# Three stages of one fused kernel: the root turned by transfers, splits ahead of squares, pooled low parts on GpSimd, two heads' values in streams of 512 columns

## What is computed

```python
def multiscale_pool(u):            # 4 groups of 128 channels, windows 2, 4, 8, 16
    ...
    return window_sum / count - ug

def second_block(x, norm_mix, w_in, ...):
    for l in range(DEPTH_2):
        h = rmsnorm(x, norm_mix[l])
        proj = h @ w_in[l]
        q, k, v, r, lr_f, lr_b, u, g_a, g_b = jnp.split(proj, split_points, axis=-1)
        ...
        o_fwd = gla_chunked(qh, kh, vh, af, include_diag=True)     # 4 heads, chunks of 64
        ...
        o = o * lax.rsqrt(jnp.mean(o * o, axis=-1, keepdims=True) + EPS)
        o = (o * gla_norm * jax.nn.silu(r)).astype(x.dtype)
        y_a = o @ w_branch_gla[l]
        pooled = multiscale_pool(u)
        y_b = jnp.einsum('blgc,gcd->blgd', pooled, w_pool_group[l]).reshape(bsz, length, D_MODEL)
        merged = jax.nn.sigmoid(g_a) * y_a + jax.nn.sigmoid(g_b) * (y_b * pool_scale[l])
        x = x + merged @ w_out[l]
        ...
```

## Time and profile before

| | |
|---|---|
| Median of 3 runs | 1809.94 us (1809.89 to 1810.12) |
| The profiled execution | 1811.46 us, its span 1810.2 us |
| Granted clock of the core | 0.999 |
| PE busy | 1792.0 us, 99% |
| DVE busy | 1274.1 us, 70% |
| ACT busy | 812.8 us, 45% |
| POOL busy | 291.7 us, 16% |

### The profile page before, as it was taken

One profiled execution on the slowest core, in us unless ns is written; L12 is line 12 of the kernel. 1 busy time (PEld: TensorE's weight loads), 2 busy tenths in 40 slices (PEclk: granted clock), 3 DMA queues, 4 the chain that ended last, 5 costly groups with the idle time before them and its releaser, 6 DMA issues.

```text
span 1810.2 us, 21907 instructions
## 1 busy us (share of the span) xinstructions
PE 1792.0 (99%) x8576; PEld 1459.0 (81%) x8580; DVE 1274.1 (70%) x1687; ACT 812.8 (45%) x1072; POOL 291.7 (16%) x236
## 2 busy tenths in 40 slices
PE   9999999999999999999999999999999999999998
PEld 7888888888877668888888878788888888888886
DVE  7896868686879865767686887666447455856757
ACT  6753534343434863444343454566323343323334
POOL 0004000000145874000000041111001321011012
PEclk9999999999999999999999999999999999999999
DMA  6233253443234003452524222222332223431512
GB/s 234 94 117 115 72 186 79 133 133 98 65 99 140 25 1 117 136 166 47 183 54 159 61 92 76 65 70 71 96 114 82 94 93 140 140 117 47 175 59 76
DMA packets 153222, 186.39 MB, mean 103 GB/s; under 512 B 8576, under 2 KB 121344, under 8 KB 153120
## 3 DMA queue, kind: packets, MB, share of 16 engines
q1 hardware_dynamic: 144944, 166.13, 28.4%
q0 software_dynamic: 7632, 18.35, 5.0%
q10 hardware_dynamic: 544, 0.52, 0.1%
HBM read 182.71 MB, written 2.14 MB: 102 GB/s over the span
## 4 chain that ended last, share of the span: by engine, by line
PE 85%; DVE 8%; ACT 3%; issue 2%; POOL 1%; DMA 1%; another core or an unknown queue 0%; DVEq 0%; SPq 0%; ACTq 0%; POOLq 0%
PE bank L1006 26%; PE bank L1008 26%; PE bank L1007 26%; DVE wlo L2083 1%; PE bank L1227 1%; PE bank L1042 1%; DVE work L2485 1%; PE bank L1253 1%; ACT whi L1490 1%; DVE t L2482 1%; DVE XC L2180 1%; PE bank L1365 1%; PE bank L1231 0%; DVE qe L2643 0%; PE bank L1383 0%
## 5 line engine op out<-in xcount | busy, mean ns | idle before, releaser
L1006 PE MATMUL bank<-Ahi,whi 128*128 128x512 f32 x1400 | 550.7, 393 | 2.3 <-DVE wlo L2109 0.8
L1007 PE MATMUL bank<-Alo,whi 128*128 128x512 f32 x1400 | 545.7, 390 | 0.0
L1008 PE MATMUL bank<-Ahi,wlo 128*128 128x512 f32 x1400 | 545.6, 390 | 0.0
L2083 DVE TENSOR_TENSOR wlo<-stage,whi 128x2048 fp32r<-128x2048 f32 (+1 forms) x133 | 304.7, 2291 | 174.6 <-ACT whi L1490 174.4
L1490 ACT ACTIVATE whi<-stage 128x2048 fp32r<-128x2048 f32 (+1 forms) x139 | 262.5, 1889 | 191.6 <-PE bank L1008 155.9
L1006 PEld LDWEIGHTS bank<-Ahi,whi 128*128 128x128 f32 x1400 | 262.7, 188 | 65.4 <-issue 7.9
L1007 PEld LDWEIGHTS bank<-Alo,whi 128*128 128x128 f32 x1400 | 262.7, 188 | 55.8 <-issue 1.2
L1008 PEld LDWEIGHTS bank<-Ahi,wlo 128*128 128x128 f32 x1400 | 262.6, 188 | 55.6
L1006 PE MATMUL bank<-whi,Hh 128*128 128x512 f32 x602 | 234.8, 390 | 0.0
L1008 PE MATMUL bank<-whi,Hl 128*128 128x512 f32 x602 | 234.2, 389 | 0.0
L1007 PE MATMUL bank<-wlo,Hh 128*128 128x512 f32 x602 | 234.2, 389 | 0.0
(11 more groups left out here) (366 smaller groups left out, 2481.1 us busy)
## 6 DMA issues: line engine op xcount, KB each, us to landing
stage<-in_mlp_w_up SPq DMA_DIRECT2D x32, 1024.0 KB, 5.4
stage<-in_w_in SPq DMA_DIRECT2D x22, 1024.0 KB, 5.0
stage<-in_w_ffn_in SPq DMA_DIRECT2D x22, 1024.0 KB, 4.9
quad<-in_mlp_w_down SPq DMA_DIRECT2D x16, 1024.0 KB, 7.3
stage<-in_mlp_w_down SPq DMA_DIRECT2D x16, 1024.0 KB, 5.0
quad<-in_mlp_w_down POOLq DMA_DIRECT2D x8, 1024.0 KB, 8.7
stage<-in_rec_w_in SPq DMA_DIRECT2D x6, 1024.0 KB, 5.3
stage<-in_att_w_in SPq DMA_DIRECT2D x6, 1024.0 KB, 5.1
```

Source lines behind the costliest of these rows:

```text
L1006: e.matmul(ps, hi, rh, start=first, stop=False, skip_group_check=onto)
L1007: e.matmul(ps, hi, rl, start=False, stop=False, skip_group_check=onto)
L1008: return e.matmul(ps, lo, rh, start=False, stop=last, skip_group_check=onto)
L2083: e.tensor_tensor(lo_of(u)[:, 0:nk, 0:n], source(u), f32(hi_of(u)[:, 0:nk, 0:n]), ALU.subtract).then_inc(s_lo[slot_of[u]], 1)
```

## The change

There are five edits.

1. `turn_root` and its label are gone. POOL issues four transfers from the row `rstd` to the columns of `rtok` instead, and ACT waits for them (`s_wp` 64).
2. The high and low tiles of slots 0 and 1 are declared as one pair each. `first_values` waits for V0 and V1 together, and for each of the four token blocks streams 256 columns of both: 96 matmuls of 512 columns in four bank labels `vv`, with `decays(0)` behind the first. ACT copies the first three labels, then makes the high part of Q1, then copies the fourth.
3. For heads 1, 2 and 3 ACT makes the high part of the next unit ahead of `out_squares`, and DVE its low part ahead of `out_over_root`. Head 0 is left as it was.
4. The low parts of the pool weights and of the pooled groups are made by POOL, between its loads of the counts. Semaphores are renumbered for that.
5. `turn_identity(25)` in place of 20.

The pieces of the diff stand in this order: PE at the start, the ring of labels, POOL's transfers, PE's values and their call, ACT's copies, the moved high and low parts on ACT and on DVE, and POOL's new function.

```diff
-        turn_identity(20)
+        turn_identity(25)
...
-    ring.add(("v", 0, 0), "rt", ("z", 0, 0), ("z", 0, 1))
-    pair(("V", 0), ("v", 0, 1))
-    pair(("V", 1), ("v", 1, 0), ("v", 1, 1))
+    ring.add(("vv", 0), ("z", 0, 0), ("z", 0, 1))
+    pair(("V", 0), *[("vv", j) for j in range(1, 4)])
+    u_end["V", 1] = ("vv", 3)
...
+        e.wait_ge(s_rstd, RSTD["gla"])
+        for j in range(4):
+            e.dma_start(rtok[:, j:j + 1], rstd[0:1, j * 128:(j + 1) * 128]).then_inc(s_wp, 16)
...
+        def first_values():
+            for h in range(2):
+                take_unit(("V", h))
+            for j in range(4):
+                ps = begin(("vv", j))
+                for k in range(8):
+                    t = three(ps[:, :].rearrange("p (h n) -> p h n", h=2), Ahi[:, k, j * 128:(j + 1) * 128], Alo[:, k, j * 128:(j + 1) * 128],
+                              whi_pair[:, :, k, :], wlo_pair[:, :, k, :], k == 0, k == 7)
+                t.then_inc(*ring.put(("vv", j)))
+                if j == 0:
+                    decays(0)
...
-        values(0, lambda: [turn_root(), decays(0)])
-        values(1)
+        first_values()
...
-        copy_v(0)
+        copy_first_v(0, 1, 2)
         hi(u_of["V", 1] + 1)
-        copy_v(1)
+        copy_first_v(3)
...
             if h == 0:
                 hi(u_of["K", 1] + 1)
+            elif h < 3:
+                hi(u_of["V", h + 1] + 1)
+            else:
+                hi(u_of["GA", 3] + 1)
             out_squares(h)
             if h < 3:
                 remaining(h + 1)
             out_root(h)
-            if 0 < h < 3:
-                hi(u_of["V", h + 1] + 1)
-            elif h == 3:
-                hi(u_of["GA", 3] + 1)
...
             if h == 0:
                 lo(u_of["K", 1] + 1)
+            elif h < 3:
+                lo(u_of["V", h + 1] + 1)
+            else:
+                lo(u_of["GA", 3] + 1)
             out_over_root(h)
...
+        def pooled_low(m):
+            e.wait_ge(s_mgh, 2 + m + 1)
+            e.wait_ge(s_mg, m + 2)
+            e.tensor_tensor(pooled_lo[:, m, :], pooled[:, m, :], f32(pooled_hi[m][:, :]), ALU.subtract).then_inc(s_mg, 1)
```

More of the change, by code:

```diff
@@ L970, in gpsimd_program @@
             e.dma_start(invc[:, :], I["invcount"][m:m + 1, :].broadcast_to([128, S])).then_inc(s_ic, 16)
+            if m == 0:
+                for i in range(2):
+                    e.wait_ge(s_mgh, i + 1)
+                    if i:
+                        e.wait_ge(s_mg, 1)
+                    e.tensor_tensor(w_pool_lo[:, 2 * i:2 * i + 2, :], w_pool[:, 2 * i:2 * i + 2, :], f32(w_pool_hi[i][:, :, :]), ALU.subtract).then_inc(s_mg, 1)
+            else:
+                pooled_low(m - 1)
+        pooled_low(3)
         for m in range(8):
@@ L1315, in tensor_program @@
         product(("qk", 3), s, 128, Ahi, Alo)
[L1316 to L1321, removed]
         def decays(h):
@@ L1358, in states @@
                 if g == 0 and d == 0:
-                    e.wait_ge(*ring.free(("v", h, 0)))
-                    e.wait_ge(*ring.free(("v", h, 1)))
+                    for label in (("v", h, 0), ("v", h, 1)) if h > 1 else [("vv", j) for j in range(4)]:
+                        e.wait_ge(*ring.free(label))
                 for par in range(2):
@@ L1444, in tensor_program @@
             s = take_unit(("wo2", m // 2))
-            product(("wo2", m), s, 0, MGh, MGl, ready=s_mgl if m == 0 else None, n0=5)
+            product(("wo2", m), s, 0, MGh, MGl, ready=s_mgl if m == 0 else None)
             if m == 6:
@@ L1853, in remaining, with copy_first_v @@
                 e.activation(t1_[d][:, :], t1_[d][:, :], ACT.Exp, scale=1.0 / 16).then_inc(s_exl, 1)
+        def copy_first_v(*blocks_):
+            e.wait_ge(s_wp, 64)
+            for j in blocks_:
+                label = ("vv", j)
+                e.wait_ge(*ring.full(label))
+                for h in range(2):
+                    half = slot_of[u_of["V", h]] * 256
+                    i = e.activation(V[:, h, j, :], ring.bank(label)[:, half:half + 256], ACT.Copy, scale=rtok[:, j:j + 1])
+                    if h == 0:
+                        i.then_inc(*st.inc())
+                        e.wait_ge(*st.now())
+                    else:
+                        i.then_inc(*ring.take(label))
         def copy_v(h):
-            if h == 0:
-                e.wait_ge(*ring.free("rt"))
             for jj in range(2):
@@ L2613, in vector_program @@
         lo(u_of["V", 1])
-        e.wait_ge(*ring.full("rt"))
-        e.tensor_copy(rtok[:, :], ring.bank("rt")[:, 0:4]).then_inc(*ring.take("rt"))
         def decays(h):
```

33 lines of the change are left out of this document (8 added, 25 removed).

## The result

The changed kernel took **1816.14 us** (median, 1815.6 to 1816.69) against 1810.25 us of the kernel before in the same comparison: a ratio of 1.0033, with a 95% interval from 1.0022 to 1.0044. It is slower by 5.9 us. The forecast was 1815.0 us, with a range of 1812.5 to 1818.0. The profiled execution took 1816.69 us with a span of 1815.4 us, where that of before had 1811.46 us and 1810.2 us. So the spans are 5.2 us apart, which is the forecast's 5.1; the medians are 5.9 us apart.

A forecast was written before the change was run, and what follows sets the result against it. PE, busy for 99% of the span, was taken to bound the kernel. Stage +6.6, clock +2.2, splits -1.8, pool -0.8 and start -1.1 made +5.1 us: span 1815.3, median 1815.0, range 1812.5 to 1818.0.

The forecast's parts named there:

- The stream: Values of heads 0 and 1: 96 matmuls of 512 columns cost PE less than 192 of 256; -1.2 us.
- The stand: After K0, PE waits for V1's high and low parts, since V1 takes K0's slot; +7.4 us.
- Q1, +2.7: Before Q1, PE waits for its parts, since Q1 takes V0's slot, in use until all values end; +2.7 us.
- The clock: Behind the wait for V1, PE's clock falls to half rate for some products; +2.2 us, bounds 0 and 4.6.
- the clock stays up: Rival: PE's clock does not fall behind the wait for V1; 1812.8 us, or 1813.9 without a gain at the start; 18%.
- The rival of a longer low stretch: Behind the wait for V1, the clock stays down longer, as long as from 1.75 on; +2.4 us more, 1817.4; 10%.
- The bank wait: Between the two heads' last values, PE's wait for a copy goes, the fourth label finding its bank free; -1.3 us.
- The root: Behind K0 and the first values, transfers replace PE's four small matmuls and stay hidden; -1.0 us.
- Splits: Before the products of R2 and head 3's like step, PE's waits for ACT's copy go; -1.8 us, two times 0.9.
- Pool: In the pool stage, PE's stand before `ya` 2 shrinks as POOL takes subtractions from DVE; -0.8 us, bounds 0 and -1.0.
- The start: At the kernel's start, five more identity turns fill PE's gap, so the clock rises sooner; -1.1 us, bounds -1.2 and +0.3.
- the forecast but no gain at the start: Rival: all other terms hold, but the five extra identity turns at the start bring nothing; 1816.1 us; 17%.

The follow-up runs named there:

- e1: The changed kernel with the values of heads 0 and 1 made one after the other again, in matmuls of 256 columns; 1804.6 us.
- e6: The kernel before with only the moves of high and low parts for heads 1 to 3, ahead of the squares; 1808.5 us.
- e7: The kernel before with only the low parts of the pool stage moved to POOL; 1809.12 us.
- e9: The kernel before with only the root turned by transfers, its matmuls and its bank label gone; 1808.43 us.
- e10: The kernel before with the root still turned by PE's matmuls, but into bank 7, its label out of the ring; 1808.8 us.
- e8: The changed kernel with V1 split into a third place of its own and Q1 taking the slot of K0; 1803.32 us.
- e2: The changed kernel with 64 turns of the identity on PE between K0's last product and the wait for both value units; 1814.14 us.
- e11: The changed kernel with identity turns in both stands, 64 ahead of the first values and 22 ahead of Q1's product; 1813.93 us.
- e3: The changed kernel with V1's high part on ACT and low part on DVE made earlier, shortening the stand; 1813.18 us.
- e4: The kernel before with the stream of 512 columns alone, the root still turned by PE and its label kept in the ring; 1826.53 us.
- e5: The kernel before with only 25 turns of the identity at the start in place of 20; 1811.11 us.
- e12: The kernel of e8 with 20 turns of the identity at the start instead of 25; 1803.93 us.

## Why the prediction was right, and where it wasn't

- **What bounds it.** Right. Without the added waits (e1) PE is at Q1 11.6 us earlier and the time is 11.5 us shorter. Waits taken away came out in the time too: 1.7, 1.2, 2.5 and 1.5 us by the traces of e6, e7, e9 and e10, 2.3, 1.7, 1.8 and 1.5 us by their medians.
- **The stream, -1.2.** Right in size, 1.3 by e8 against e1. The distances of starts were the right rows; the busy times would have promised 16.
- **The stand, +7.4.** 7.5. The step held because it went by the slot rule and by two rows of ACT and DVE whose own causes the edit did not touch.
- **Q1, +2.7.** 2.7 in the profile. But that DVE "just makes" what PE needs two products later was too kind: PE is 0.2 us later behind head 0's first states (8.2 us behind the kernel before instead of 8.0).
- **The clock, +2.2.** 2.6, inside its bounds. e2 and e11 put 2.0 to 2.2 us on it in medians. The rival "the clock stays up" falls with the profile and e2; in every profile the clock fell behind the stands of 4.4 us and more (the changed kernel, e3, twice in e4). The rival of a longer low stretch (+2.4 more) did not happen.
- **The bank wait, -1.3.** Right as a number, wrong in its cause. I wrote that it goes "since the fourth label finds its bank free", and counted that to the stage of the stream. It is free because the root's label left the ring (e10: -1.5 us with the stream absent). With the label kept, the stream turns 1.2 us into 4.7 (e4). By my terms the stream alone would cost 7.4 + 2.7 - 1.2 - 1.3 + 2.2 = 9.8 us; e4 showed 1826.53 - 1810.78 = 15.8.
- **The root, -1.0.** -0.94 on PE; with the label 2.5 us in the trace. The transfers were hidden, as said: in the profile after, POOL issues them from 1080.93 to 1083.16, each lands 2.0 us later, and ACT's first copy of values is at 1111.21.
- **Splits, -1.8.** Right, -1.8 in the profile and -1.7 in e6, though the copy was only one of two things that PE waited for.
- **Pool, -0.8.** -1.2, 0.2 past its better bound. Of the stretched DVE work I took 2.1 us as given back; it was 1.0 for each of two groups, as foreseen. But the stand of 1.0 us went in full, and with it 0.1 to 0.2 us behind it that I had not counted: the products right after a wait start further apart (1371.46, 1371.80, 1372.04 in the kernel before, where 0.2267 is usual).
- **The start, -1.1.** -0.96 in the profile and nothing in the median (e5). This is the step that failed. I derived it from a single profiled execution with a late clock, then moved the sum to the median, which seems to belong to executions that mostly had the early clock already (four of seven profiles with 20 turns have it; the timed runs have no trace). The rows were right; that the execution was 1.5 us above its median was a hint I used for the level and not for the term. Without the term the forecast is 1816.1, which is the rival "the forecast but no gain at the start" and the time measured. That it agrees to the tenth is luck: the clock came out 0.4 us dearer and the pool stage 0.4 us cheaper than their terms.

The sum by the trace: -1.0 (start) + 8.9 (stage) + 0.2 (behind head 0's first states) - 1.8 - 1.2 = +5.1, against spans 5.2 us apart. In medians it is 5.9, as before's usual execution is shorter than its profiled one.

## What to carry over

Joining two units of weights into one wider stream asks for both at once, so look first at when the second one's place comes free; here the stream was worth 1.2 us, and its wait with all that followed 13, until the second unit had a place of its own. A label in a ring of banks is a resource like an engine: count how many places back a bank was last used before you price the matmuls that use it. And before a term is taken from one profiled execution, ask whether that execution is like the median, above all for what happens in its first ten microseconds.

## What the runs showed of the hardware

- The granted clock of PE fell to 0.50 (1.2 GHz) in the profiles behind stands of 4.4, 4.7 and 7.5 us in the middle of a kernel that had run at 1.00 for a millisecond. Behind 7.5 us 24 products of 512 columns lost 2.6 us, behind 4.4 us 2.9: in these profiles the price did not grow with the stand.
- A wait of 2.5 us went both ways: the clock fell behind it in the profile of e2 and not in those of the changed kernel and of e3. Filled with turns of the identity (e11) it takes the spread of the runs from 2.0 to 0.6 us.
- With the same 20 turns the clock was up at the first product or 3.3 to 3.7 us later (e7, before and e9), by the distances of starts; the granted clock is recorded as 1.00 all the while. The Trainium skill, "TensorE: Matmul & The Clock Gate", "Part 1: The HAM clock gate", says that the number of slow matmuls at a kernel's start varies from run to run, and the profiles with 20 turns agree: none slow in e4, e6, e10 and e12, eight in e7, nine in before and in e9.
- 64 turns of the identity, 7.15 us of them, kept the clock up (e2, e11): the products behind them are 0.23 us apart.
